# Both head pairs of a mixer as one unit of work in the three smallest query tiles of prompt attention

## The chip, the core and the metric

The kernel runs on one core of a Trainium2 chip (trn2). The metric is the device time of one execution in microseconds (us). The core has five engines that run beside each other and meet at semaphores: TensorE (PE in the profile, with its weight loads as PEld), VectorE (DVE), ScalarE (ACT), GpSimd (POOL) and SyncE (SP), which here only issues transfers.

## The reference, cut to what matters

The program is one decoder layer for a prompt of 1024 tokens and for 8 requests of 8 new tokens each. The change lies in the attention of the prompt, which has four branches. Three are those of a sparse attention with 8 query heads on 2 key heads, whose outputs are summed with gates, and the fourth is a forgetting attention with 8 heads of its own:

```python
def block(args):                       # one query tile of 128 rows
    o_n = nsa_block(...)               # g0 * compressed + g1 * selected + g2 * window
    o_f = fox_block(...)               # softmax(q k^T * scale + cq - ck) v, causal
...
lc = einsum(q, kc) * scale + bias      # compressed keys, one for 16 tokens      -> branch CMP
ls = einsum(q, kg) * scale + bias      # selected blocks (16 of 16: all)         -> branch SLC
lw = einsum(q, kw) * scale + bias      # the last 512 keys                       -> branch WIN
```

Each branch is a masked softmax over the keys up to the query, followed by a product with the values. Everything is float32.

## The kernel before, in words

`prompt_attention` handles the 1024 prompt rows in 8 query tiles of 128 rows. Query tile i needs (i + 1) * 128 keys in SLC and FOX, at most 640 in WIN, and 8i + 7 compressed keys in CMP. The tiles are not taken in the order of their number but as `TILE_ORDER = (6, 0, 5, 1, 4, 2, 3, 7)`, and all of it is done twice, in two turns of four heads per key head side: so the tiles 0, 1 and 2, the smallest three, come up six times.

The unit of work is a `Pair`: one query tile, one branch and one head pair j (0 or 1), of which `half` 0 and 1 are the two heads, on array rows 0 to 63 and 64 to 127. A tile has eight pairs, always as `CMP 0, SLC 0, SLC 1, WIN 0, CMP 1, WIN 1, FOX 0, FOX 1`; 128 pairs in all. Each goes through these steps:

- `scores` (L799, PE): one matmul for each half and 512 columns, into PSUM. A half owns two banks; a pair of at most 512 columns takes one of them, alternating with the number of the pair, and a wider one (`wide`) takes both. The score matmuls wait for the logits of all pairs up to the one before the last, or, if this pair or the one before is wide, up to the last.
- `logits` (L912; for FOX L899 for all but the diagonal 128 columns and L902 for those, with a wait between, DVE): adds the bias and takes the minimum of the negated row, for each half.
- `exps` (L956, ACT): exponential with the row sum, for each half.
- `invert` (L918, L920, DVE): the reciprocals of the sums.
- normalisation (L1021, POOL): the probabilities times the reciprocal and the gate, for each half. Ahead of WIN 0, POOL also adds the causal mask to the diagonal of the FOX bias (L1003).
- `turn` (L811, PE): transposes of 128 columns each, up to four into one of the three banks 4, 5 and 7; a pair of up to four key tiles is one chunk, a larger one two.
- `save` (L965 on ACT for half 0, L928 on DVE for half 1): the transposed probabilities to SBUF.
- `weighted_values` (L840 for CMP, SLC and WIN, both head pairs at once, 256 columns; L831 for FOX, for each head pair): the products with the values into bank 6, in two parts, one and two pairs behind the second pair of the branch. `save_out` (L972, L974, ACT) takes the results away.

The order is written out by hand. In iteration p each engine does a fixed list, in this order:

```python
# PE:   turn(p, 0); scores(p + 3); values of the pairs p - 2 and p - 1; turn(p, 1)
# DVE:  save(p, 0); logits(p + 3); save(p, 1); invert(p + 2)
# ACT:  save(p, 0); exps(p + 2, 1); save(p, 1); exps(p + 3, 0); save_out(p - 2)
# POOL: for each p in turn: wait for inverse_ready of p, normalise half 0, normalise half 1
wait_for = p.n if p.wide or (p.n and PAIRS[p.n - 1].wide) else p.n - 1     # scores
pe.wait_ge(logits_done, 2 * wait_for)
pe.wait_ge(normed, 2 * p.n + half + 1)                                     # turn
```

Transfers for the next stage, the attention of the requests, are issued by SP when the logits of the last tile (7) of the second turn are done (`logits_done`).

Of the kernel before, what the change touches and what calls it, by code (L numbers as in the profile page):

```python
# [7 lines left out]
ALU = mybir.AluOpType  # L8
ACT = mybir.ActivationFunctionType

P = 128
D = 1024
KD = D // P
T = 1024
# [7 lines left out]
NTP = T // P  # L22
# [70 lines left out]
class EarlyLayout:  # L93


    def __init__(self, arena):
# [21 lines left out]
        self.nmax, self.sums = view(arena, 24256, 4, 2, 2), view(arena, 24272, 4, 2)  # L118
# [519 lines left out]
class Pair:  # L638


    def __init__(self, n, turn, i, branch, j):
        self.n, self.turn, self.i, self.branch, self.j = n, turn, i, branch, j
        self.g = 2 * turn + j
        done = self.done = turn * NTP + TILE_ORDER.index(i)
        self.group = 4 * done + GROUPS.index(branch)
# [20 lines left out]
ORDER = ((CMP, 0), (SLC, 0), (SLC, 1), (WIN, 0), (CMP, 1), (WIN, 1), (FOX, 0), (FOX, 1))  # L666
GROUPS, BIG = (SLC, CMP, WIN, FOX), (SLC, WIN, FOX)
PAIRS = [Pair((t * NTP + y) * 8 + x, t, i, br, j)
         for t in range(2) for y, i in enumerate(TILE_ORDER) for x, (br, j) in enumerate(ORDER)]
NPAIR, AHEAD, VALUES_BEHIND = len(PAIRS), 3, 2  # L670
TURNED_BEFORE = [sum(len(q.chunks) for q in PAIRS[:n]) for n in range(NPAIR + 1)]
FOX_SPLITS = [sum(q.branch == FOX and q.i > 0 for q in PAIRS[:n]) for n in range(NPAIR + 1)]
# [10 lines left out]
def pair_no(turn, i, branch, j):  # L683
    return (turn * NTP + TILE_ORDER.index(i)) * 8 + ORDER.index((branch, j))


def prompt_attention(k, keep, io):
# [5 lines left out]
    with ExitStack() as local:  # L693
# [26 lines left out]
        def probs_of(p, half, s=0, w=None):  # L720
            return (probs_cmp if p.branch == CMP else probs)[:, p.slot, half, s:s + (p.width if w is None else w)]

        def turned_of(p):
            return (probsT_cmp if p.branch == CMP else probsT)[:, p.buf]

# [3 lines left out]
        def _(sp):  # L729
            sp.dma_start(causal[:], io["c_causal"]).then_inc(mask_in, 16)  # L730
            for turn in range(2):
                if turn:
                    sp.wait_ge(logits_done, 2 * pair_no(0, LAST_TILE, CMP, 1) + 2)
                    slc_bias(sp, at, io, turn, slc_in)
                if turn:
                    sp.wait_ge(logits_done, 2 * pair_no(0, LAST_TILE, WIN, 1) + 2)
# [4 lines left out]
                if turn:  # L741
                    sp.wait_ge(logits_done, 2 * pair_no(0, LAST_TILE, FOX, 1) + 2)
# [29 lines left out]
            sp.wait_ge(logits_done, 2 * pair_no(1, LAST_TILE, CMP, 1) + 2)  # L772
            compressor_weights(sp, ahead, io, keep.cw_in)
            sp.wait_ge(logits_done, 2 * pair_no(1, LAST_TILE, WIN, 1) + 2)
            for p in range(4):
                key_pages(sp, ahead, io, keep.first_ids, 0, p, keep.k_in)
            sp.wait_ge(logits_done, 2 * NPAIR)
# [4 lines left out]
        def _(pe):  # L782
            def scores(p):
                wait_for = p.n if p.wide or (p.n and PAIRS[p.n - 1].wide) else p.n - 1
                if wait_for > 0:
                    pe.wait_ge(logits_done, 2 * wait_for)
                pieces = split(p.width)
                for s, w in pieces:
                    cols = slice(p.k0 + s, p.k0 + s + w)
                    for half in range(2):  # L790
                        rows = slice(half * HD, (half + 1) * HD)
                        q = (keep.qfT if p.branch == FOX else keep.qT)[rows, p.g, p.i * P:(p.i + 1) * P]
                        if p.branch == FOX:
                            keys = keep.fkT[rows, p.g, cols]
# [4 lines left out]
                        mm = pe.matmul(scores_at(p, half, s, w), q, keys, start=True, stop=True)  # L799
                        if s + w == p.width:  # L800
# [1831 lines left out]
```

## Time and profile before

| | us |
|---|---|
| median of 3 runs (2605.86 to 2613.88) | 2608.65 |
| the profiled execution | 2611.62 |
| span of the profiled execution | 2609.8 |
| prompt attention inside it | about 341 to 744 |

The times of instructions below are microseconds from the start of the span. A row of the timeline gives the start, the duration, the engine, the line of the kernel, the operation with its operands and how many instructions it covers, and in brackets the idle time of the engine just before it and what ended that. A float32 matmul is recorded as several instructions: the score matmul of one piece of up to 512 columns for both halves is x4, and a transpose is x1. What an engine needs for a group is best read as the step from its start to the start of the next group, since the ends of matmuls overlap. The granted clock of TensorE is 0.998 of full speed over the span (2.4 GHz).

### The profile page before, as it was taken

What the parts mean: (1) busy time and instruction counts of PE and PEld (TensorE: products, weight loads), DVE (VectorE), ACT (ScalarE), POOL (GpSimd) and SP (SyncE); (2) the same over time, 40 slices, a digit from 0 to 9 for tenths busy, and PEclk for the clock granted to TensorE, in tenths of its full rate; (3) what the DMA queues carried; (4) which work ended last, traced back from release to release, by engine and by line L of the source; (5) the groups of instructions that cost most, each with busy time, mean ns of one, the idle gap of its engine ahead of it and who ended that gap; (6) DMA issues with size and microseconds to landing.
All of it is one profiled execution on the core that took longest, in us unless ns stands there. A gap on an engine that the chain in (4) does not pass through costs nothing.

```text
span 2609.8 us, 29562 instructions
## 1 busy us (share of the span) xinstructions
PE 2544.0 (97%) x10607; PEld 1400.4 (54%) x10607; DVE 974.1 (37%) x2734; ACT 521.0 (20%) x1306; POOL 356.3 (14%) x561
## 2 busy tenths in 40 slices
PE   9999999999989999999999999999999999999999
PEld 4554655565556675666664455555555554443443
DVE  5874246767743331101016722222222210407312
ACT  0001036656633331000002211101010110101110
POOL 0000025445540001000003400000000000202100
PEclk9999999999999999999999999999999999999999
DMA  5325430030088766111304111111111214323300
GB/s 184 93 75 174 155 123 1 1 129 2 5 209 246 223 199 202 41 32 35 102 5 95 41 33 32 43 38 32 32 32 48 78 56 162 105 97 130 127 32 32
DMA packets 198931, 227.17 MB, mean 87 GB/s; under 512 B 52551, under 2 KB 150279, under 8 KB 197263
## 3 DMA queue, kind: packets, MB, share of 16 engines
q1 hardware_dynamic: 192226, 199.85, 25.6%
q0 software_dynamic: 5424, 16.28, 1.8%
q10 hardware_dynamic: 1168, 9.58, 1.2%
q8 instruction: 65, 1.06, 0.2%
q14 instruction: 48, 0.39, 0.0%
HBM read 203.60 MB, written 37.99 MB: 93 GB/s over the span
## 4 chain that ended last, share of the span: by engine, by line
PE 61%; DVE 0%; ACT 0%; issue 0%; DVEq 0%
PE ps L2114 25%; PE ps L2164 12%; PE ps L2072 9%; PE ps L2195 5%; PE ps L2065 5%; PE ps L2092 4%; PE ps L2168 1%; PE ps L2198 0%; PE ps L2096 0%; PE ps L2121 0%; PE ps L2054 0%; PE ps L2103 0%; DVE arena L2425 0%; DVE qfT L2442 0%; ACT arena L2300 0%
## 5 line engine op out<-in xcount | busy, mean ns | idle before, releaser
L2114 PE MATMUL ps<-xT,qT 128*128 128x480 f32 (+1 forms) x2112 | 647.9, 469 | 0.0
L2114 PEld LDWEIGHTS ps<-xT,qT 128*128 128x128 f32 x2112 | 344.6, 191 | 297.6 <-issue 297.6
L2164 PE MATMUL ps<-arena 128*128 128x512 f32 x704 | 305.1, 594 | 0.0
L2072 PE MATMUL ps<-xT,arena 128*128 128x363 f32 (+1 forms) x768 | 238.1, 467 | 0.0
L2164 PEld LDWEIGHTS ps<-arena 128*128 128x128 f32 x704 | 132.8, 190 | 171.1 <-issue 170.8
L236 PE MATMUL ps<-arena,xT 128*128 128x512 f32 (+1 forms) x512 | 198.9, 551 | 1.3 <-issue 0.8
L2373 DVE TENSOR_SCALAR qfT<-qfT 128x480 f32<-128x480 f32 (+1 forms) x88 | 35.1, 420 | 435.3 <-ACT qfT L2252 435.3
L2072 PEld LDWEIGHTS ps<-xT,arena 128*128 128x128 f32 x768 | 145.4, 189 | 88.8
L956 ACT ACTIVATE arena<-arena 128x640 f32<-128x640 f32 (+15 forms) x256 | 164.8, 644 | 66.2 <-DVE arena L912 46.2
L236 PEld LDWEIGHTS ps<-arena,xT 128*128 128x128 f32 x512 | 98.1, 192 | 101.8 <-issue 94.2
L811 PE MATMUL ps<-ident,arena 128*128 128x128 f32 (+4 forms) x880 | 137.7, 284 | 10.9 <-POOL arena L1021 5.1
L1021 POOL TENSOR_SCALAR arena<-arena,gates 128x55 f32<-128x55 f32 (+15 forms) x192 | 122.8, 649 | 174.0 <-DVE arena L920 173.8
L2344 DVE TENSOR_TENSOR arena<-arena,ps 128x726 f32<-128x726 f32 (+1 forms) x24 | 21.9, 911 | 319.4 <-ACT arena L2233 319.4
L811 PEld LDWEIGHTS ps<-ident,arena 128*128 128x128 f32 (+4 forms) x880 | 91.6, 138 | 68.2 <-POOL arena L1021 29.9
L153 DVE STREAM_TRANSPOSE xT<-arena 32x256 f32<-32x256 f32 x256 | 111.6, 436 | 8.7 <-DMA arena<-in_x_all 4.8
L2195 PE MATMUL ps<-arena,xT 128*128 128x512 f32 x256 | 112.8, 593 | 0.0
L912 DVE CUSTOM_DVE_ANT_0 arena<-ps,arena 128x55 f32<-128x55 f32 (+15 forms) x192 | 96.1, 538 | 41.5 <-PE ps L799 40.5
L2092 PE MATMUL ps<-arena 128*128 128x512 f32 x256 | 110.3, 593 | 0.0
L2252 ACT COPY qfT<-ps 128x480 f32<-128x480 f32 x44 | 24.6, 558 | 427.9 <-PE ps L2114 427.9
L928 DVE COPY xT<-ps 128x512 f32<-128x512 f32 (+11 forms) x176 | 85.3, 484 | 52.0 <-PE ps L811 50.6
L799 PE MATMUL ps<-arena,qT 64*128 64x512 f32 (+11 forms) x512 | 87.5, 439 | 14.0 <-DVE arena L912 12.0
L1450 PE MATMUL ps<-ident,arena 128*128 128x128 f32 x556 | 77.5, 280 | 20.4 <-DMA arena<-in_cache_fox_kv 10.9
(288 smaller groups left out, 2594.2 us busy)
## 6 DMA issues: line engine op xcount, KB each, us to landing
arena<-in_w_ffn_down SPq DMA_DIRECT2D x66, 512.0 KB, 3.5
arena<-in_cache_fox_kv SPq DMA_DIRECT2D x72, 256.0 KB, 5.8
xT<-in_cache_fox_kv SPq DMA_DIRECT2D x56, 256.0 KB, 7.2
arena<-in_cache_nsa_kv SPq DMA_DIRECT2D x64, 192.0 KB, 4.5
qT<-in_w_ffn_up SPq DMA_DIRECT2D x22, 512.0 KB, 4.0
qT<-in_w_ffn_gate SPq DMA_DIRECT2D x22, 512.0 KB, 5.2
bias_rows<-rev_dram ACTq DMA_DIRECT2D x8, 1160.0 KB, 30.2
arena<-in_w_in SPq DMA_DIRECT2D x16, 512.0 KB, 5.4
```

Of the source, the lines that this page charges most:

```text
L153: ins = nc.vector.transpose(out[q * 32:(q + 1) * 32, :, z * 32:(z + 1) * 32], rows[z * 32:(z + 1) * 32, :].rearrange("p (c w) -> p c w", c ...
L236: mm = pe.matmul(ps[:, bank_of(i, n), 0:b - a], keep.xT[:, c, t0:t0 + m], w_rows[:, c, a:b], start=(c == 0), stop=(c == KD - 1))
L811: mm = pe.transpose(ps[0:w, turn_bank(p, c, half), x * P:(x + 1) * P], probs_of(p, half, s, w), keep.ident[:])
L912: nc.vector.tensor_tensor_reduce(dst, scores_at(p, half), bias, -1.0, FLOOR, ALU.add, ALU.min, low).then_inc(logits_done, 1)
L956: nc.scalar.activation(x, x, ACT.Exp, bias=nmax[:, p.n % 4, half, 0:1], scale=-1.0, accum_out=sums[:, p.n % 4, half:half + 1]).then_inc(ex ...
L1021: nc.gpsimd.tensor_scalar(x, x, sums[:, p.n % 4, half:half + 1], gate, ALU.mult, ALU.mult).then_inc(normed, 1)
L2065: pe.matmul(ps[:, 4 * (j % 2) + 2 + side, 0:n], at.w_branch[e][:, side, c, :], o[:, c, t0:t0 + n], start=(c == 0), stop=(c == 3))
L2072: mm = pe.matmul(ps[:, 4 * (j % 2) + side, 0:n], at.w_gate[e][:, side, c, :], x[:, c, t0:t0 + n], start=(c == 0), stop=(c == KD - 1))
L2092: mm = pe.matmul(ps[:, q + n, :], mergedT[:, c, t0:t0 + m], at.w_out[:, c, cols], start=(c == 0), stop=(c == KD - 1))
L2114: mm = pe.matmul(ps[:, 2 * (j % 3) + side, 0:n], at.w_ug[e][:, side, c, :], x[:, c, t0:t0 + n], start=(c == 0), stop=(c == KD - 1))
L2164: mm = pe.matmul(ps[:, q + h, :], hT[:, c, t0:t0 + m], at.w_down[:, load % RING, cols], start=(c == 0), stop=(c == NFF - 1))
L2195: mm = pe.matmul(ps[:, o, :], src[:, c, t0:t0 + m], w[:, c, cols], start=(c == 0), stop=(c == kk - 1))
```

## The change

In the query tiles 0, 1 and 2 the two head pairs of a branch become one `Unit`; the other tiles keep one head pair per unit, in the old order. A small tile is now four units, `CMP, SLC, WIN, FOX`, and there are 104 units in place of 128 pairs. In a unit of both head pairs:

- the score matmuls of both are issued one after the other, and `scores_ready` is counted up for a half behind the second head pair. The number of matmuls stays. Up to 256 columns a head pair (tiles 0 and 1, and CMP) both share one bank of a half; above that (SLC, WIN and FOX of tile 2, with 384 columns) the unit is `wide`, with a bank for each head pair and half, so all four banks.
- logits, exponentials and normalisations are as many as before, with one count of the semaphore for each half and not for each head pair; the guard and the reciprocal of the sums are one for both.
- a chunk of transposes is up to two key tiles of both head pairs: one chunk in the tiles 0 and 1, two (two key tiles, then one) in tile 2. A save copies both head pairs.
- the values are multiplied whole, not in two parts: CMP two units behind, the others one unit behind, and `save_out` follows one unit behind.
- CMP comes first of its tile and so opens the accumulation in bank 6.

The look-ahead stays three units, so in a small tile the scores of the next large tile are issued two or three units before it.

```diff
-class Pair:
-
...
-            self.slot, self.buf, self.freed = j, done % 2, self.group - 8 + 1
+            self.buf, self.freed = done % 2, group_no(done - 2, CMP) + 1
         else:
...
-            self.slot = (6 * done + 2 * big + j) % 3
+            self.slot = bigs % 3
             self.buf = (3 * done + big) % 2
-            before = GROUPS.index(BIG[big - 2]) + 4 * (done - (big < 2))
-            self.freed = before + 1
+            self.freed = group_no(done - (big < 2), BIG[big - 2]) + 1
         self.tiles = [(self.k0 // P + t, s, w) for t, (s, w) in enumerate(split(self.width, P))]
-        self.wide = self.width > 512
-        self.chunks = split(len(self.tiles), 4)
+        self.wide = self.width > (256 if self.both else 512)
+        self.chunks = split(len(self.tiles), 2 if self.both else 4)
...
-ORDER = ((CMP, 0), (SLC, 0), (SLC, 1), (WIN, 0), (CMP, 1), (WIN, 1), (FOX, 0), (FOX, 1))
-GROUPS, BIG = (SLC, CMP, WIN, FOX), (SLC, WIN, FOX)
-PAIRS = [Pair((t * NTP + y) * 8 + x, t, i, br, j)
...
+SINGLE = ((CMP, (0,)), (SLC, (0,)), (SLC, (1,)), (WIN, (0,)), (CMP, (1,)), (WIN, (1,)), (FOX, (0,)), (FOX, (1,)))
+DOUBLE = ((CMP, (0, 1)), (SLC, (0, 1)), (WIN, (0, 1)), (FOX, (0, 1)))
+BIG = (SLC, WIN, FOX)
+
+
+def groups_of(i):
+    return (CMP, SLC, WIN, FOX) if i < 3 else (SLC, CMP, WIN, FOX)
+
...
+    for t in range(2):
+        for i in TILE_ORDER:
+            for branch, heads in (DOUBLE if i < 3 else SINGLE):
+                units.append(Unit(len(units), t, i, branch, heads, bigs))
+                bigs += branch != CMP
+    return units
...
+WHOLE_BEHIND, HALVES_BEHIND = {CMP: (2,), SLC: (1,), WIN: (1,), FOX: (1,)}, (1, 2)
+def values_behind(p):
+
+    return WHOLE_BEHIND[p.branch] if p.both else HALVES_BEHIND
...
-        def scores_at(p, half, s=0, w=None):
-            base = half * 1024 + (0 if p.wide else (p.n % 2) * 512)
+        def scores_at(p, half, j, s=0, w=None):
+            base = half * 1024 + (0 if p.wide else (p.n % 2) * 512) + (j * (512 if p.wide else 256) if p.both else 0)
...
+        def probs_of(p, half, j, s=0, w=None):
+            w = p.width if w is None else w
+            if p.branch == CMP:
+                return probs_cmp[:, j, half, s:s + w]
+            s += 512 * j if p.both else 0
+            return probs[:, p.slot, half, s:s + w]
...
+        def turned_rows(p, t0, m, w, half):
+            heads = slice(p.heads[0], p.heads[-1] + 1)
+            return turned_of(p)[0:w, t0:t0 + m, half, heads, :].rearrange("p t j q -> p t (j q)")
+
+        def turned_bank(p, c, m, w, half):
+            return ps[0:w, turn_bank(p, c, half), 0:m * len(p.heads) * P].rearrange("p (t x) -> p t x", t=m)
...
-                wait_for = p.n if p.wide or (p.n and PAIRS[p.n - 1].wide) else p.n - 1
+                wait_for = p.n if p.wide or (p.n and UNITS_P[p.n - 1].wide) else p.n - 1
...
+                pieces = [(j, s, w) for j in p.heads for s, w in split(p.width)]
+                for j, s, w in pieces:
...
+                        mm = pe.matmul(scores_at(p, half, j, s, w), q, keys, start=True, stop=True)
+                        if (j, s, w) == pieces[-1]:
                             mm.then_inc(scores_ready, 1)
...
+                    for x, ((kt, s, w), j) in enumerate((tile, j) for tile in p.tiles[t0:t0 + m] for j in p.heads):
+                        mm = pe.transpose(ps[0:w, turn_bank(p, c, half), x * P:(x + 1) * P], probs_of(p, half, j, s, w), keep.ident[:])
...
-                cut = (last + 2) // 2
+                cut = last + 1 if p.both else (last + 2) // 2
                 some = list(enumerate(p.tiles))[part * cut:(part + 1) * cut]
+                heads = (0, 1) if p.both else (part,)
...
                         pe.wait_ge(nsa_saved, done + 1)
-                    for j in (part,):
+                    for j in heads:
...
-                    if p.branch == SLC and part == 0 and done:
+                    opens = p.branch == groups_of(p.i)[0]
+                    if opens and part == 0 and done:
                         pe.wait_ge(fox_saved, done)
...
                                            turned[0:w, x, half].rearrange("p j q -> p (j q)"),
-                                           start=(p.branch == SLC and x == 0), stop=(p.branch == WIN and x == last))
-                if part == 1 if p.branch == FOX else some[-1][0] == last:
+                                           start=(opens and x == 0), stop=(p.branch == WIN and x == last))
+                if heads[-1] == 1 if p.branch == FOX else some[-1][0] == last:
                     mm.then_inc(pv_done, 1)
...
             def values_beside(n):
-                for part in (1, 0):
-                    q = n - 1 - part
-                    if 0 <= q < NPAIR and PAIRS[q].j == 1:
-                        weighted_values(PAIRS[q], part)
+                for behind in (2, 1):
+                    q = UNITS_P[n - behind] if 0 <= n - behind < NUNIT else None
+                    if q and q.last and behind in values_behind(q):
+                        weighted_values(q, values_behind(q).index(behind))
...
+                    for x, j in enumerate(p.heads):
+                        dst = probs_of(p, half, j)
+                        low, part = nmax[:, p.n % 4, half, x, 0:1], nmax[:, p.n % 4, half, x, 1:2]
...
+                                dve.wait_ge(half_max, FOX_SPLITS[p.n] + len(p.heads) * half + x + 1)
...
+                    ins.then_inc(logits_done, 1)
...
+                nc.vector.tensor_copy(turned_rows(p, t0, m, w, 1), turned_bank(p, c, m, w, 1)).then_inc(saved_b, 1)
...
+                for n, j in enumerate(p.heads):
+                    x = probs_of(p, half, j)
+                    ins = nc.scalar.activation(x, x, ACT.Exp, bias=nmax[:, p.n % 4, half, n, 0:1], scale=-1.0,
+                                               accum_out=sums[:, p.n % 4, half, n:n + 1])
+                ins.then_inc(exp_done, 1)
...
+                nc.scalar.copy(turned_rows(p, t0, m, w, 0), turned_bank(p, c, m, w, 0)).then_inc(saved_a, 1)
...
+                for behind in (2, 1):
+                    q = UNITS_P[p.n - behind] if p.n >= behind else None
+                    if q and q.last and q.branch in (WIN, FOX) and values_behind(q)[-1] == behind:
+                        save_out(q)
...
+                    for n, j in enumerate(p.heads):
+                        x = probs_of(p, half, j)
+                        column = half * 12 + (2 * p.turn + j) * 3 + p.branch
+                        gate = 1.0 if p.branch == FOX else keep.gates[:, p.i, column:column + 1]
+                        ins = nc.gpsimd.tensor_scalar(x, x, sums[:, p.n % 4, half, n:n + 1], gate, ALU.mult, ALU.mult)
+                    ins.then_inc(normed, 1)
```

## Rows read from the trace of the kernel before

**Rows 1.** Busy time by stage: us, engines, granted clock, DMA share, GB/s.

```profile
341.50:744.40 402.90, 376.79 (x2800) 224.30 (x2800) 275.65 (x1058) 244.52 (x722) 191.00 (x281) 1.00 0.17 56
389.60:399.70 10.10, 9.77 (x102) 6.58 (x102) 6.66 (x45) 6.91 (x35) 6.26 (x14) 1.00 0.01 2
...
475.58:494.46 18.88, 18.75 (x141) 10.22 (x141) 14.78 (x63) 12.80 (x43) 10.21 (x17) 1.00 0.00 1
...
745.00:800.00 55.00, 46.59 (x358) 35.02 (x356) 14.99 (x27) 14.83 (x25) 20.54 (x51) 0.97 0.96 239
```

**Rows 2.** Timeline of PE, query tile 0 into tile 5, first turn.

```profile
390.34 1.75 PE L831 MATMUL ps<-xT,arena 128*64 128x128 f32 x28
392.02 0.44 PE L811 MATMUL ps<-ident,arena 128*128 128x128 f32 x2
...
394.39 0.44 PE L811 MATMUL ps<-ident,arena 128*128 128x128 f32 x2
394.76 0.49 PE L799 MATMUL ps<-arena,qT 64*128 64x128 f32 x4
395.18 0.44 PE L811 MATMUL ps<-ident,arena 128*128 128x128 f32 x2
...
399.33 0.44 PE L811 MATMUL ps<-ident,arena 128*128 128x128 f32 x2
399.70 1.56 PE L799 MATMUL ps<-arena,qT 64*128 64x512 f32 x8
...
403.19 1.56 PE L799 MATMUL ps<-arena,qT 64*128 64x512 f32 x8 [0.98 <-DVE arena L912]
...
406.68 1.35 PE L799 MATMUL ps<-arena,qT 64*128 64x512 f32 x8 [1.58 <-DVE arena L912]
```

**Rows 3.** Timeline of PE, query tile 1 into tile 4, first turn.

```profile
432.97 0.70 PE L799 MATMUL ps<-arena,qT 64*128 64x256 f32 x4
433.60 1.53 PE L831 MATMUL ps<-xT,arena 128*64 128x128 f32 x24
...
438.66 0.66 PE L811 MATMUL ps<-ident,arena 128*128 128x128 f32 x4
439.24 0.70 PE L799 MATMUL ps<-arena,qfT 64*128 64x256 f32 x4
...
444.79 1.35 PE L799 MATMUL ps<-arena,qT 64*128 64x512 f32 x8
...
447.81 1.35 PE L799 MATMUL ps<-arena,qT 64*128 64x512 f32 x8 [0.49 <-DVE arena L912]
...
450.82 1.35 PE L799 MATMUL ps<-arena,qT 64*128 64x512 f32 x8 [0.74 <-DVE arena L912]
```

**Rows 4.** Timeline of PE, query tile 2 into tile 3, first turn.

```profile
475.78 0.92 PE L799 MATMUL ps<-arena,qT 64*128 64x384 f32 x4
...
491.68 0.87 PE L811 MATMUL ps<-ident,arena 128*128 128x128 f32 x6
492.49 1.13 PE L799 MATMUL ps<-arena,qT 64*128 64x512 f32 x4
...
494.46 1.13 PE L799 MATMUL ps<-arena,qT 64*128 64x512 f32 x4
```

**Rows 5.** Timeline of DVE, tile 2: logits of one pair, then of FOX.

```profile
482.00 0.56 DVE L912 CUSTOM_DVE_ANT_0 arena<-ps,arena 128x384 f32<-128x384 f32 x1 [0.28 <-PE ps L799]
...
482.48 0.55 DVE L912 CUSTOM_DVE_ANT_0 arena<-ps,arena 128x384 f32<-128x384 f32 x1
...
483.91 0.42 DVE L899 CUSTOM_DVE_ANT_0 arena<-ps,arena 128x256 f32<-128x256 f32 x1
...
484.65 0.42 DVE L899 CUSTOM_DVE_ANT_0 arena<-ps,arena 128x256 f32<-128x256 f32 x1
```

**Rows 6.** Timeline of POOL, tile 2: the diagonal and a normalisation.

```profile
479.42 1.27 POOL L1003 TENSOR_TENSOR arena<-arena 128x512 f32<-128x512 f32 x1
481.02 1.30 POOL L1021 TENSOR_SCALAR arena<-arena,gates 128x384 f32<-128x384 f32 x2 [0.33 <-DVE arena L920]
```

More of the change, by code:

```diff
@@ L635, in _, with __init__ @@
             nc.vector.tensor_copy(keep.vc[0:CMP_N, :], ps[0:CMP_N, HIGH, HD:HD + P]).then_inc(kcvc_saved, 1)
-class Pair:
-    def __init__(self, n, turn, i, branch, j):
-        self.n, self.turn, self.i, self.branch, self.j = n, turn, i, branch, j
-        self.g = 2 * turn + j
+class Unit:
+    def __init__(self, n, turn, i, branch, heads, bigs):
+        self.n, self.turn, self.i, self.branch, self.heads = n, turn, i, branch, heads
+        self.both, self.first, self.last = len(heads) == 2, heads[0] == 0, heads[-1] == 1
         done = self.done = turn * NTP + TILE_ORDER.index(i)
-        self.group = 4 * done + GROUPS.index(branch)
+        self.group = group_no(done, branch)
         if branch == CMP:
             self.k0, self.width = 0, 8 * i + 7
-            self.slot, self.buf, self.freed = j, done % 2, self.group - 8 + 1
+            self.buf, self.freed = done % 2, group_no(done - 2, CMP) + 1
         else:
@@ new lines, in group_no, with units_in_order @@
+def group_no(done, branch):
+    return 4 * done + groups_of(TILE_ORDER[done % NTP]).index(branch)
+def units_in_order():
+    units, bigs = [], 0
+    for t in range(2):
[4 more added lines that the diff above has]
+    return units
+UNITS_P = units_in_order()
+NUNIT, AHEAD = len(UNITS_P), 3
+TURNED_BEFORE = [sum(len(q.chunks) for q in UNITS_P[:n]) for n in range(NUNIT + 1)]
@@ L675 @@
+FOX_SPLITS = [sum(2 * len(q.heads) for q in UNITS_P[:n] if q.branch == FOX and q.i > 0) for n in range(NUNIT + 1)]
+WHOLE_BEHIND, HALVES_BEHIND = {CMP: (2,), SLC: (1,), WIN: (1,), FOX: (1,)}, (1, 2)
+def values_behind(p):
+    return WHOLE_BEHIND[p.branch] if p.both else HALVES_BEHIND
 TURN_BANKS = (4, 5, 7)
@@ L680, in turn_bank, with unit_no @@
     return TURN_BANKS[(2 * (TURNED_BEFORE[p.n] + c) + half) % 3]
-def pair_no(turn, i, branch, j):
-    return (turn * NTP + TILE_ORDER.index(i)) * 8 + ORDER.index((branch, j))
+def unit_no(turn, i, branch, j):
+    return next(q.n for q in UNITS_P if (q.turn, q.i, q.branch) == (turn, i, branch) and j in q.heads)
 def prompt_attention(k, keep, io):
@@ L791, in scores @@
                         rows = slice(half * HD, (half + 1) * HD)
-                        q = (keep.qfT if p.branch == FOX else keep.qT)[rows, p.g, p.i * P:(p.i + 1) * P]
+                        q = (keep.qfT if p.branch == FOX else keep.qT)[rows, g, p.i * P:(p.i + 1) * P]
                         if p.branch == FOX:
-                            keys = keep.fkT[rows, p.g, cols]
+                            keys = keep.fkT[rows, g, cols]
                         elif p.branch == CMP:
@@ L867, in _ @@
             pe.wait_ge(queries_b, 1)
[L868 removed]
+            for p in UNITS_P:
                 if p.n == 1:
@@ L885, in logits @@
                     if p.branch in (SLC, CMP):
-                        dve.wait_ge(slc_in[p.j], 32 * p.turn + 32)
-                    elif p.j == 0:
+                        for j in p.heads:
+                            dve.wait_ge(slc_in[j], 32 * p.turn + 32)
+                    elif p.first:
                         dve.wait_ge(win_in if p.branch == WIN else fox_in, 64 * p.turn + 64)
-                if p.j == 0 and p.branch == FOX:
+                if p.first and p.branch == FOX:
                     dve.wait_ge(diag_ready, p.done + 1)
@@ L1001, in set_diagonal @@
                 if p.done % NTP >= 2:
-                    pool.wait_ge(logits_done, 2 * pair_no(p.turn, TILE_ORDER[p.done % NTP - 2], FOX, 1) + 2)
+                    pool.wait_ge(logits_done, 2 * unit_no(p.turn, TILE_ORDER[p.done % NTP - 2], FOX, 1) + 2)
                 nc.gpsimd.tensor_tensor(diag_fox[:, p.done % 2], bias_fox[:, :, :, p.i * P:(p.i + 1) * P].rearrange("p h j n -> p (h j) n"),
@@ L1013, in _ @@
             pool.wait_ge(mask_in, 16)
-            for p in PAIRS:
-                if p.branch == WIN and p.j == 0:
+            for p in UNITS_P:
+                if p.branch == WIN and p.first:
                     set_diagonal(p)
```

130 lines of the change are left out of this document (50 added, 80 removed).

## The prediction

> **What bounds the kernel now.** I read the busy time by stage first, then the timeline of PE around each small tile, then DVE's and POOL's for the steps that PE might wait for. In the busy times the reader is to see that prompt attention takes 402.9 us, that PE is busy in 376.79 of them, and that in tile 0 it is so for 9.77 of 10.10 us and in tile 2 for 18.75 of 18.88 us, at a granted clock of 1.00 (2.4 GHz) [rows 1]. DVE, the next, has 14.78 of 18.88 us. So the small tiles are bound by PE, and a part of PE's time is the price of small groups. The exception is the end of the tiles 0 and 1: there PE issues the scores of the next large tile, which take all score banks, and stands 0.98 and 1.58 us, or 0.49 and 0.74 us, waiting for DVE's logits [rows 2, 3]. Nothing stands there in tile 2, since tile 3 has 512 columns and its scores alternate between banks [rows 4].
>
> **Length of the small tiles.** SLC(5) is SLC of tile 5, and so on. Take as the end of a tile the start of the third large score group behind it. From the first scores issued in the tile's CMP 0 that is 450.82 - 432.97 = 17.85 us for tile 1 [rows 3] and 494.46 - 475.78 = 18.68 us for tile 2 [rows 4]; in tile 0 those scores come one step of 0.42 us ahead of the FOX values at 390.34, so 406.68 - 389.9 = 16.8 us [rows 2].
>
> **What the change does to PE's steps.** Nothing of the matrix work goes; a group's fixed part goes. A group's step is its duration less some 0.07 us.
> - Scores: 128 columns of one head pair step 0.42 us (394.76 to 395.18) [rows 2]. What a piece of 128 more columns adds shows between 256 and 384 columns, 0.92 - 0.70 = 0.22 us [rows 3, 4]. A unit of two is thus 0.42 + 0.21 = 0.63 against 0.84 us, and so with 256 columns (0.63 + 0.43 = 1.06 against 1.26) and 384 (0.85 + 0.64 = 1.49 against 1.70). With CMP some 0.8 us a tile.
> - Transposes: two step 0.37 us (394.39 to 394.76) [rows 2], four 0.58 (438.66 to 439.24) [rows 3], six 0.81 (491.68 to 492.49) [rows 4]: 0.11 each and 0.15 for the group. Four groups less in the tiles 0 and 1: 0.6 us. In tile 2 a big unit has two chunks (eight and four), 1.03 + 0.58 = 1.61 against 2 x 0.81, so nothing but 0.15 for CMP.
> - Values: no longer split, 0.1 us a group; 0.2 to 0.3 us in tile 2.
> That is 1.4 us of PE's work in tiles 0 and 1 and some 1.2 us in tile 2.
>
> **What it does to the waits.** Half the iterations mean that the scores of the next tile come earlier against the small tile's remaining work. For tile 0, from the rows, PE is busy back to back. The prefetched scores of three units make CMP's turn later by about 0.5 us, at 390.2. Then: turn CMP 0.5, scores FOX 0.65, values of FOX(6) 1.68 (390.34 to 392.02) [rows 2], turn SLC 0.58, scores CMP(5) 0.33, values 1.68, turn WIN 0.58: SLC(5)'s scores start at 396.2 to 396.4 against 399.70. The next two follow at the distance that DVE's logits set, 3.49 us (399.70 to 403.19) [rows 2]. PE's own work between them, 1.49 scores, 1.1 values of CMP and SLC, 0.58 transposes of FOX, is 3.2 us and just fits. The third is at 403.4 against 406.68: **3.25 us** gained, 1.4 of fixed parts, 1.3 of the wait at the end and the rest short waits inside the tile, which PE no longer meets.
>
> Tile 1, in the same way: CMP turn at about 433.1, then 0.7, 1.06, 1.46 (432.97 group's values, 433.60, less 0.07) [rows 3], 1.03, 0.33, 1.46 and WIN's transposes. Here the transposes wait for POOL. Its normalisation of SLC ends near 436.3, the diagonal takes 1.27 [rows 6], and four normalisations of WIN at 0.55 end near 440.1 (0.55 is an estimate between 0.65 for 384 columns [rows 6] and the shorter ones). SLC(4)'s scores start at 440.65. Now PE itself sets the distance: 1.28 + 1.6 values + 1.03 transposes = 3.9 us, then 3.02 (444.79 to 447.81) [rows 3]: third group at 447.6 against 450.82, **3.2 us**.
>
> Tile 2 is the doubtful one. Its SLC, WIN and FOX scores fill all four banks, so each must wait until the last one's logits are done. DVE needs 0.48 us for each head and head pair, 1.93 for the unit (482.00 to 482.48), for FOX 0.74 and 2.96 (483.91 to 484.65) [rows 5]. On PE the values and transposes behind a score group cover it: behind SLC's 2.8 us, of tile 4 (covered); behind WIN's 1.8 us (a wait of about 0.2 us); behind FOX's 2.3 us, values 1.25 and transposes 1.03 (a wait of about 0.7 us). These three are my counts of groups by the steps above. DVE's queue costs more: `invert` of WIN stands behind the logits of FOX and comes at 482.3, POOL then takes 2 x 1.30 [rows 6], and PE has WIN's second half of transposes at 484.95, some 0.4 us late. Without any wait the tile would be 16.7 us: 18.68 less 1.2 of fixed parts and less 0.7 of short waits for POOL inside it, such as the 0.3 us that end at each normalisation. Of the new waits some hide each other; I take 0.8 us, so 17.5 against 18.68: **1.2 us** gained. Bounds: 2.0 gained with no wait, 4.9 lost (second rival).
>
> Saves: one of 512 columns for two of 256; they and the exponentials lie on ACT beside PE (6.91 of 10.10 us busy in tile 0 [rows 1]) and cost nothing on the path; were they bare, ACT in tile 2 would be 12.8 of 17.5 us, still no bound. The longer hand-over (a half is announced after both head pairs) is in the schedule above; POOL's queue holds only the next units behind it. No DMA is issued in another place; SP's waits keep their events.
>
> **Behind the stage.** The loads of the next stage are issued on the logits of the last tile, and until then DMA is at 0.17 of its time [rows 1]. The 55 us that follow are bound by DMA at 0.96, which starts with those issues; so the gain is passed on, since everything slides.
>
> **Sum.** 2 turns x (3.25 + 3.2 + 1.2) = 15.3 us. The profiled execution is 2611.62 (span 2609.8 and 1.8 around it), 3.0 over the median: 2611.62 - 15.3 = 2596.3 for a like execution, and 2608.65 - 15.3 = **2593.4** for the median.
>
> **Rivals.**
> 1. *The small tiles gain in part.* If the waits inside tiles 0 and 1 come back (POOL's four normalisations of a unit in a row, against two now) but the fixed parts go, it is 2 x (1.4 + 1.4 + 0) = 5.6: 2603. For it: POOL ended idle times of PE already in these tiles. Against: POOL has 6.26 of 10.10 us busy [rows 1].
> 2. *All four banks give up the overlap.* If nothing covers the logits, tile 2 has PE idle for 1.93 + 1.93 + 2.96 = 6.8 us, less 1.2 of work and 0.7 of waits that go: 4.9 lost, so 2 x (6.45 - 4.9) = 3.1 gained, 2605.5. For it: this is just how PE stands at the large tiles [rows 2]. Against: there PE had too little other work; here it has. The Trainium skill (Perfetto Trace Analysis, Matmuls) says that independent matmul groups should rotate through PSUM banks so that the eviction of one overlaps the next; by that rule, which speaks against the wide units, this rival would be the likely one. The trace agrees with it at tile 5.
> 3. *Slower: the ring of a wide unit closes.* In tile 2 each unit runs turn 1.03, scores 1.49, logits 2.96, the second turn and save 1.0, invert 0.4, normalisation 2.6 one behind the other: 9.5 us where two pairs take 4.6. Three such units lose 14.7 us a turn: 29.4 less 12.9 of the other tiles, 16.5 slower, 2625. It decides from a loss of 2.2 us for each wide unit on. Against it: the look-ahead of three units, which lets the steps of neighbours lie beside each other.
> 4. *Absorbed.* The stage behind waits for something that does not slide (a load issued early): 2608. Against: DMA's mean share of 0.17 in this stage [rows 1], and loads that are issued by its last tile.
>
> **Chances.** Forecast 0.74, rival 1 0.07 and rival 2 0.07, rival 3 0.07, rival 4 0.05. About 0.3% (7.8 us) is what a measurement of this kernel can tell from none. Rivals 1, 2 and 4 lie within it, 0.19; from their edges 0.01 goes to either side: faster 0.75, same 0.17, slower 0.08. The forecast's own range reaches 2 x 0.8 us further down for tile 2 and 2 x 1.3 for the waits for POOL and for PE's own distance in tile 1, and some 6 us up, if each small tile meets one more wait of 1 us: 2589 to 2600. To leave out no more than 2 in 10 it takes in rivals 1 and 2: **2587 to 2606**.
>
> **What would show it.** In the trace of the changed kernel: score groups x8 of 2 x 128 columns stepping about 0.63 us; the score group of tile 5 at 3.2 us earlier against tile 0's start, tile 4's likewise; idle time of PE before WIN's and FOX's scores in tile 2 of a few tenths, against 2 us in rival 2; PE's second half of WIN's transposes released by POOL in tile 2. Wrong would be the forecast if PE stood over 1 us before each wide group of tile 2, if POOL ended more than 1.5 us of idle time in tile 0 or 1, or if the stage behind did not start earlier by 15 us.

## The result, and the profile after

| | median us | ratio to before, 95% interval |
|---|---|---|
| before (13 runs beside it) | 2611.07 | |
| the changed kernel (13 runs) | 2616.72 | 1.0019 [1.0012, 1.0027] |

The change made the kernel slower by 0.19%, 5.65 us, where 15.3 us less were forecast. It is within the 0.3% called no difference ahead, but the interval lies clear of 1. The profiled execution took 2616.97 us with a span of 2615.2 us, at a mean granted clock of 0.993 against 0.998.

The stage as a whole, then stretches in the tiles 1 and 2 of the first turn, with the columns of [rows 1]:

```profile
341.00:744.00 403.00, 368.09 (x2720) 225.90 (x2718) 259.50 (x991) 237.53 (x701) 190.58 (x279) 0.97 0.16 53
...
434.00:442.00 8.00, 5.97 (x73) 4.55 (x70) 4.58 (x27) 5.05 (x19) 4.19 (x7) 1.00 0.01 2
442.00:448.00 6.00, 5.21 (x26) 2.73 (x28) 2.26 (x6) 2.02 (x9) 3.22 (x7) 0.72 0.01 3
481.60:486.40 4.80, 1.22 (x12) 0.84 (x8) 2.88 (x17) 1.43 (x5) 1.74 (x2) 0.83 0.00 0
486.40:491.80 5.40, 5.33 (x36) 4.84 (x36) 1.79 (x12) 2.92 (x10) 3.06 (x5) 0.52 0.01 3
```

PE was busy in 1.22 of the 4.80 us from 481.6 us on, and then 5.33 of 5.40 us at a clock of 0.52: it first stood and then worked at half speed (1.2 of 2.4 GHz; the clock had already fallen within the wait, at about 484.7). In tile 1 the same follows in small. Nowhere in this stage does the kernel before show a clock under 1.00 [rows 1].

PE's timeline shows both at the instruction (in the changed kernel L837 are the scores, L849 the transposes, L870 the values of FOX, L880 the other values). In tile 1 of the changed kernel:

```profile
438.56 1.53 PE L870 MATMUL ps<-xT,arena 128*64 128x128 f32 x24
442.38 0.66 PE L849 MATMUL ps<-ident,arena 128*128 128x128 f32 x4 [2.29 <-POOL arena L1065]
443.45 0.86 PE L849 MATMUL ps<-ident,arena 128*128 128x128 f32 x4 [0.42 <-POOL arena L1065]
444.25 2.50 PE L837 MATMUL ps<-arena,qT 64*128 64x512 f32 x8
```

The same timeline of the changed kernel in tile 2:

```profile
478.97 1.56 PE L837 MATMUL ps<-arena,qfT 64*128 64x384 f32 x8
480.46 1.31 PE L870 MATMUL ps<-xT,arena 128*64 128x128 f32 x20
481.70 1.11 PE L849 MATMUL ps<-ident,arena 128*128 128x128 f32 x8
486.47 0.64 PE L837 MATMUL ps<-arena,qT 64*128 64x31 f32 x4 [3.65 <-DVE arena L943]
487.04 2.40 PE L870 MATMUL ps<-xT,arena 128*64 128x128 f32 x20
489.37 2.57 PE L849 MATMUL ps<-ident,arena 128*128 128x128 f32 x12
491.87 1.13 PE L837 MATMUL ps<-arena,qT 64*128 64x512 f32 x4
```

In tile 1 PE waits 2.29 us for POOL's normalisation of WIN, and the score group behind it takes 2.50 us where its like takes 1.35 [rows 3]. In tile 2 it waits 3.65 us for the last FOX logits (L943), and the values and transposes behind take 2.40 and 2.57 us. Who was late there is on two more timelines of the changed kernel. POOL's:

```profile
479.50 2.60 POOL L1065 TENSOR_SCALAR arena<-arena,gates 128x384 f32<-128x384 f32 x4 [2.80 <-DVE arena L961]
482.07 1.27 POOL L1045 TENSOR_TENSOR arena<-arena 128x512 f32<-128x512 f32 x1
486.82 2.60 POOL L1065 TENSOR_SCALAR arena<-arena,gates 128x384 f32<-128x384 f32 x4 [3.48 <-DVE arena L961]
```

And DVE's:

```profile
483.37 0.42 DVE L940 CUSTOM_DVE_ANT_0 arena<-ps,arena 128x256 f32<-128x256 f32 x1 [3.65 <-POOL arena L1045]
...
486.53 0.18 DVE L961 RECIPROCAL arena<-arena 128x4 f32<-128x4 f32 x1
```

The FOX scores were ready at 480.53, but DVE began their logits at 483.37, released by POOL's L1045: 2.8 us late. That line adds the causal mask to the diagonal of the FOX bias, and it stands in POOL's queue between SLC's four normalisations and WIN's. Before, FOX 0's logits came in the iteration of WIN 0, when the diagonal was done: in tile 2 at 480.69, and the logits began at 483.91 [rows 5, 6]. In a tile of four units they come in CMP's iteration. DVE stands 2.8 to 3.7 us for it in each of the six small tiles and in no large one; `invert` of WIN is queued behind the logits, and so POOL begins WIN at 486.8. POOL itself stands idle for 3.48 us between the diagonal and WIN, so it is not the 1.27 us of POOL's own time that make WIN late, but DVE's wait for them.

**Length by tile.** The save of the sparse branches (L972 before, L1013 now) of each large tile bounds a small one and the large one behind it. From ACT's timeline of the kernel before (tiles 6, 5, 4 and 3 of the first turn):

```profile
389.83 0.36 ACT L972 COPY qT<-ps 128x256 f32<-128x256 f32 x1
...
433.02 0.36 ACT L972 COPY qT<-ps 128x256 f32<-128x256 f32 x1
...
475.94 0.36 ACT L972 COPY qT<-ps 128x256 f32<-128x256 f32 x1
...
518.87 0.35 ACT L972 COPY qT<-ps 128x256 f32<-128x256 f32 x1
```

The same saves of the changed kernel:

```profile
393.77 0.35 ACT L1013 COPY qT<-ps 128x256 f32<-128x256 f32 x1
...
435.10 0.35 ACT L1013 COPY qT<-ps 128x256 f32<-128x256 f32 x1
...
479.56 0.35 ACT L1013 COPY qT<-ps 128x256 f32<-128x256 f32 x1
...
524.97 0.35 ACT L1013 COPY qT<-ps 128x256 f32<-128x256 f32 x1
```

| us, from save to save | before | changed | diagonal early (first run below) |
|---|---|---|---|
| with tile 0 (6 to 5) | 43.19 | 41.33 | 40.07 |
| with tile 1 (5 to 4) | 42.92 | 44.46 | 40.47 |
| with tile 2 (4 to 3) | 42.93 | 45.41 | 40.86 |

A row holds the small tile and the large one behind it, and in the large one the scores of the next small tile are prefetched. So what tile 2's prefetched scores cost, 1.9 us in tile 4 (25.06 before, 26.97 changed), stands in the row of tile 1, which without them is 0.4 us shorter than before and not 1.5 longer. To this comes 0.84 us a turn, ahead of the first save, for tile 0's scores, now issued for both head pairs (29.21 us from tile 7 to tile 6 before, 30.05 now). So a turn is 3.0 us longer and both 6.0, which is the 5.65 us of the medians.

### The profile page after: what moved, and what is told of

The parts are those of the page before. It is cut to its first block, busy times and chain, and to the rows that moved or that the text cites. A ratio compares the mean times of both kernels' runs of the same rounds, so it can differ in the third digit from the quotient of the medians.

```text
span 2615.2 us, 29416 instructions
## 1 busy us (share of the span) xinstructions
PE 2544.2 (97%) x10607; PEld 1409.7 (54%) x10607; DVE 959.8 (37%) x2668; ACT 515.5 (20%) x1288; POOL 356.9 (14%) x561
## 4 chain that ended last, share of the span: by engine, by line
PE 61%; DVE 0%; ACT 0%; issue 0%; DVEq 0%
PE ps L2159 25%; PE ps L2209 12%; PE ps L2117 9%; PE ps L2240 5%; PE ps L2110 5%; PE ps L2137 4%; PE ps L2213 1%; PE ps L2243 0%; PE ps L2141 0%; PE ps L2166 0%; PE ps L2099 0%; PE ps L2148 0%; DVE arena L2470 0%; DVE qfT L2487 0%; ACT arena L2345 0%
## 5 line engine op out<-in xcount | busy, mean ns | idle before, releaser
L849 PE MATMUL ps<-ident,arena 128*128 128x128 f32 (+4 forms) x880 | 134.0, 286 | 17.6 <-POOL arena L1065 13.2
L849 PEld LDWEIGHTS ps<-ident,arena 128*128 128x128 f32 (+4 forms) x880 | 94.1, 141 | 64.7 <-issue 28.7
L837 PE MATMUL ps<-arena,qT 64*128 64x512 f32 (+11 forms) x512 | 85.9, 445 | 16.6 <-DVE arena L943 7.8
```

Source lines behind the costliest of these rows:

```text
L849: mm = pe.transpose(ps[0:w, turn_bank(p, c, half), x * P:(x + 1) * P], probs_of(p, half, j, s, w), keep.ident[:])
```

## The experiments

Each ratio is against the kernel before, run on the same chip in the same rounds; its median was 2612.93 us beside the early diagonal, both kernels with two tiles and the early diagonal in pairs, 2611.60 beside the filled wait, the doubled, the late and the everywhere early diagonal, and 2613.17 beside the last two.

**Diagonal early in the small tiles.**

```diff
-                if p.branch == WIN and p.first:
+                if p.first and p.branch == (CMP if p.both else WIN):
                     set_diagonal(p)
```

> The changed kernel with one edit: in the small tiles POOL adds the mask to the FOX diagonal ahead of the normalisation of CMP, not ahead of that of WIN. Theory D (the FOX logits of a small tile, now issued in CMP's iteration, stand behind POOL's normalisation of SLC and the diagonal; DVE's wait of 2.8 to 3.7 us holds up the inverse of WIN and PE, and PE's idle time lets its clock fall): the six waits of DVE go, no stretch of the small tiles is at half clock, and the time falls to the forecast, about 2596 us against 2611 for the kernel before. Rival B (the four score banks of tile 2 give up the overlap): PE still stands over 2 us before the scores behind FOX in tile 2 and its clock still falls there; only the tiles 0 and 1 gain, about 2604 us. Rival C (two normalisations more in a row on POOL are what PE waits for): time stays within 3 us of the changed kernel's 2616.7.

Measured 2597.08 us against 2612.93, ratio 0.9940 [0.9926, 0.9954]: 15.85 us faster than before. DVE waits for POOL's diagonal nowhere, and no small tile has a fall of the clock (all lengths stand in the table above). PE's timeline of this kernel in tile 2:

```profile
474.55 1.10 PE L849 MATMUL ps<-ident,arena 128*128 128x128 f32 x8
476.62 0.41 PE L837 MATMUL ps<-arena,qT 64*128 64x31 f32 x4 [0.97 <-DVE arena L943]
476.96 1.31 PE L870 MATMUL ps<-xT,arena 128*64 128x128 f32 x20
478.20 1.09 PE L849 MATMUL ps<-ident,arena 128*128 128x128 f32 x8
479.60 0.66 PE L849 MATMUL ps<-ident,arena 128*128 128x128 f32 x4 [0.31 <-POOL arena L1065]
480.19 1.13 PE L837 MATMUL ps<-arena,qT 64*128 64x512 f32 x4
```

From POOL's and DVE's timelines of the same kernel, the normalisation of SLC and the first of FOX's logits:

```profile
472.35 2.59 POOL L1065 TENSOR_SCALAR arena<-arena,gates 128x384 f32<-128x384 f32 x4 [2.80 <-DVE arena L961]
...
473.52 0.42 DVE L940 CUSTOM_DVE_ANT_0 arena<-ps,arena 128x256 f32<-128x256 f32 x1 [0.95 <-PE ps L837]
```

The logits of FOX start at 473.52, released by the scores and not by POOL, a microsecond after POOL has begun SLC. PE's wait for the last of them is 0.97 us, not 3.65. Theory D stands; rival B wanted over 2 us there, and rival C the old time.

At the end of tile 0 PE's wait for the score banks is shorter than before, but not gone. PE's timeline of this kernel:

```profile
400.75 1.56 PE L837 MATMUL ps<-arena,qT 64*128 64x512 f32 x8 [0.18 <-DVE arena L953]
...
404.24 1.35 PE L837 MATMUL ps<-arena,qT 64*128 64x512 f32 x8 [1.00 <-DVE arena L953]
```

These are 0.18 and 1.00 us for 0.98 and 1.58 [rows 2]; at the end of tile 1 it is none and 0.31 us for 0.49 and 0.74 [rows 3].

**Units of both head pairs in the tiles 0 and 1 alone, with the late and with the early diagonal.**

```diff
-            for branch, heads in (DOUBLE if i < 3 else SINGLE):
+            for branch, heads in (DOUBLE if i < 2 else SINGLE):
...
-    return (CMP, SLC, WIN, FOX) if i < 3 else (SLC, CMP, WIN, FOX)
+    return (CMP, SLC, WIN, FOX) if i < 2 else (SLC, CMP, WIN, FOX)
```

> The changed kernel, but only the tiles 0 and 1 have units of both head pairs; tile 2 is as before, and no unit takes four banks at 384 columns. Theory D: tile 2 gives back the 2.5 us a turn that it lost, tile 0 still gains 1.9 and tile 1 still loses 1.5 with its fall of the clock: 2609 to 2612 us, no difference to before that can be told. Rival B (the four banks are the cause of the loss): all of the loss goes and the tiles 0 and 1 show their gain, 2603 us or less. Rival C: like theory D.

> Both edits: units of both head pairs in the tiles 0 and 1 alone, and the diagonal ahead of CMP there. Theory D: 2 x (3.25 + 3.2) = 12.9 us faster than before, 2598 us, some 2 us slower than with three tiles and the early diagonal. Rival B: the same 2598, but faster than with three tiles by 5 us or more. Rival C: near the run with two tiles and the late diagonal, 2610 us.

Measured 2608.80 us, ratio 0.9987 [0.9978, 0.9996], and 2598.63 us, ratio 0.9945 [0.9933, 0.9957]. The first is 4 us faster than before, and 8 us faster than the changed kernel; the second cannot be told from the run with three tiles (2597.08). So the tiles 0 and 1 give all of the gain, if the diagonal is early, and the four banks of tile 2 are by themselves neither the loss nor a gain. The late one missed its expectation, if narrowly: it was to show no difference to before, and its interval lies just clear of 1. The expectation charged tile 1 with the 1.9 us that tile 2's prefetched scores cost in tile 4, and they are gone here: by the saves tile 1's row is 0.4 us shorter than before in the first turn and 2.0 in the second.

The late diagonal also showed, unplanned, what the clock costs. The wait of tile 1 is the same in both turns, 2.25 us; behind it the clock fell in the first and not in the second. PE's timeline of the kernel with two tiles and the late diagonal, in both turns:

```profile
442.52 0.66 PE L849 MATMUL ps<-ident,arena 128*128 128x128 f32 x4 [2.25 <-POOL arena L1065]
443.59 0.84 PE L849 MATMUL ps<-ident,arena 128*128 128x128 f32 x4 [0.41 <-POOL arena L1065]
444.36 2.51 PE L837 MATMUL ps<-arena,qT 64*128 64x512 f32 x8
...
449.66 1.35 PE L837 MATMUL ps<-arena,qT 64*128 64x512 f32 x8
...
632.62 0.66 PE L849 MATMUL ps<-ident,arena 128*128 128x128 f32 x4 [2.25 <-POOL arena L1065]
633.69 0.66 PE L849 MATMUL ps<-ident,arena 128*128 128x128 f32 x4 [0.41 <-POOL arena L1065]
634.28 1.35 PE L837 MATMUL ps<-arena,qT 64*128 64x512 f32 x8
...
638.17 1.35 PE L837 MATMUL ps<-arena,qT 64*128 64x512 f32 x8
```

From the transposes to the second score group it is 449.66 - 442.52 = 7.14 us in the one and 638.17 - 632.62 = 5.55 us in the other: 1.6 us for one fall.

**PE's wait filled.** The changed kernel, in which SLC's first chunk of transposes is done again, into the same bank:

```diff
-                    for x, ((kt, s, w), j) in enumerate(...):
-                        mm = pe.transpose(...)
+                    for again in range({1: 3, 2: 4}.get(p.i, 1) if p.both and p.branch == SLC and c == 0 else 1):
+                        for x, ((kt, s, w), j) in enumerate(...):
+                            mm = pe.transpose(...)
                     mm.then_inc(turned, 1)
```

> The changed kernel with PE's wait filled: in the tiles 1 and 2 the first chunk of SLC's transposes is done three (tile 1) or four times (tile 2) and counted once, about 1.8 and 2.7 us of PE's work inside waits of 2.3 and 3.7 us. It does not shorten the wait's end. Theory D with the clock: the four stretches at half clock go, and with them the 1.6 us (tile 1) and 2.3 us (tile 2) that they cost a turn: 7.8 us faster than the changed kernel, 2609. Rival (the clock costs nothing, since PE would wait anyway, or the filling delays what comes after): the same as the changed kernel or slower, 2617 to 2622.

Measured 2611.26 us, ratio 0.9999 [0.9991, 1.0008]: 5.5 us faster than the changed kernel, with more work on PE. No stretch of the small tiles is at half clock. PE's timeline of this kernel in tile 2:

```profile
478.74 3.71 PE L850 MATMUL ps<-ident,arena 128*128 128x128 f32 x32
483.52 0.41 PE L837 MATMUL ps<-arena,qT 64*128 64x31 f32 x4 [1.07 <-DVE arena L944]
483.86 1.31 PE L871 MATMUL ps<-xT,arena 128*64 128x128 f32 x20
485.11 1.09 PE L850 MATMUL ps<-ident,arena 128*128 128x128 f32 x8
```

DVE's wait is still 3.66 us and PE still stands until the logits come, but only 1.07 us in one piece, and the values and transposes behind take 1.31 and 1.09 us. By the saves, the stretch with tile 1 is 1.6 us shorter and that with tile 2 1.8: 6.8 us in both turns against 7.8 expected. The rest of what the late diagonal costs, 2611.3 - 2597.1 = 14 us by the medians (12.8 by the saves), is standing time, as far as these two runs divide it.

**The diagonal twice.** The suspected cost doubled in the changed kernel:

```diff
+                nc.gpsimd.tensor_tensor(diag_fox[...], bias_fox[...], causal[...], ALU.add).then_inc(diag_first, 1)
+                pool.wait_ge(diag_first, p.done + 1)
                 nc.gpsimd.tensor_tensor(diag_fox[...], bias_fox[...], causal[...], ALU.add).then_inc(diag_ready, 1)
```

> The changed kernel with the diagonal's addition done twice in a row on POOL, in all 16 tiles. Theory D: DVE's waits for it in the six small tiles grow by 1.3 us each, some 4.1 to 5.0 us, all of it on the path in the tiles 1 and 2 and most of it in tile 0, and no stretch at half clock goes: 6 to 10 us slower than the changed kernel, 2623 to 2627. If the diagonal were beside the path (rival C), no more than 2 us.

Measured 2641.75 us, ratio 1.0111 [1.0095, 1.0126]: 25 us slower than the changed kernel, where 6 to 10 were expected. The waits of DVE did grow as expected, to 4.17, 4.48 and 5.00 us. Most of the surplus lies where I had not looked: in the large tiles PE waits for POOL's normalisation of WIN 0, behind the diagonal, as well, and in the tiles 4 and 3 the clock now falls there too. PE's timeline of this kernel in tile 4:

```profile
468.58 0.66 PE L850 MATMUL ps<-ident,arena 128*128 128x128 f32 x4 [1.14 <-POOL arena L1070]
469.44 0.66 PE L850 MATMUL ps<-ident,arena 128*128 128x128 f32 x4 [0.20 <-POOL arena L1070]
470.02 2.34 PE L838 MATMUL ps<-arena,qfT 64*128 64x512 f32 x8
472.29 2.17 PE L881 MATMUL ps<-xT,arena 128*64 128x256 f32 x12
```

The stretches from a small tile's save to that of the large tile behind it are 1.3 to 2.9 us longer each, 6.8 a turn. The small tiles' own are 1.4 to 3.3 us longer, where the wait alone grew by 1.3; in tile 1 of the first turn the clock stays at half from about 446.3 to 456.7.

**Pairs only, with a late diagonal.** The kernel before, no unit of two head pairs:

```diff
-                if p.branch == WIN and p.j == 0:
+                if p.branch == WIN and p.j == 1:
```

> The kernel before, pairs alone, with the diagonal two pairs later, ahead of WIN 1's normalisation. FOX 0's logits, issued in WIN 0's iteration, then stand behind two normalisations that were not ahead of them. Theory D: DVE waits for POOL in all 16 tiles and the kernel gets slower without any unit of two head pairs, by about 1 us a tile or more, 2625 to 2650, with stretches at half clock in the small tiles. Rival (it takes the longer units and the halved number of iterations to make that wait bare): within 3 us of before.

Measured 2644.27 us, ratio 1.0122 [1.0106, 1.0138]. DVE waits 1.5 to 1.9 us for POOL in all 16 tiles, as in tile 5 on DVE's timeline of this kernel:

```profile
424.49 0.82 DVE L899 CUSTOM_DVE_ANT_0 arena<-ps,arena 128x640 f32<-128x640 f32 x1 [1.53 <-POOL arena L1003]
```

The clock falls in five of the six small tiles. The flaw is one of order and needs no unit of two.

**The diagonal early in the kernel before, and in all tiles of the changed one.** In both the diagonal goes ahead of CMP's normalisation everywhere (`p.branch == CMP`).

> The kernel before with the diagonal moved ahead of the normalisation of CMP 0 in all tiles. Theory D: DVE never waited for it here, since FOX 0's logits come in the iteration of WIN 0; the time stays within 3 us of before, 2608 to 2614. Rival E (its place costs the kernel before as well, and a gain of the first run would not be the changed kernel's): faster than before by 5 us or more.

> The changed kernel with the diagonal ahead of CMP's normalisation in all 16 tiles, not in the small ones alone. Theory D: DVE waits for it nowhere; the large tiles never waited for it, but POOL's queue is freer ahead of WIN 0, where PE waited for POOL by some tenths: 0 to 4 us faster than with the early diagonal in the small tiles alone (2597), that is 2593 to 2597. Against: 1.3 us ahead of CMP 0 and SLC 0 might delay those, then up to 3 us slower.

Measured 2609.36 us, ratio 0.9987 [0.9979, 0.9996], and 2596.72 us, ratio 0.9942 [0.9929, 0.9955]. The first is 3.6 us faster than before, a little more than the 3 us allowed: the diagonal's place cost the kernel before a little, but not what the first run gained. By the saves only the tiles 2 and 3 are shorter there, 0.6 us a turn. The second cannot be told from the first run; in its trace only the large tile 3 is 0.9 us shorter a turn (24.49 to 23.57).

**Tile 2 alone, with the early diagonal there.**

```diff
-            for branch, heads in (DOUBLE if i < 3 else SINGLE):
+            for branch, heads in (DOUBLE if i == 2 else SINGLE):
...
-                if p.branch == WIN and p.first:
+                if p.first and p.branch == (CMP if p.both else WIN):
```

> Units of both head pairs in tile 2 alone, with the diagonal ahead of CMP there; all else as before. The forecast's term for this tile is 1.2 us a turn, so 2.4 us faster than before, 2609. By the traces of the runs with two and with three tiles it is 0.2 us a turn: no difference to before. Rival B (four banks without overlap): slower by 5 us or more, 2617.

Measured 2612.28 us against 2613.17, ratio 0.9997 [0.9988, 1.0006]: no difference. From save to save, tile 4 is 1.9 us longer (25.06 to 26.96), tile 2 2.8 shorter (19.16 to 16.38), and tile 3 0.7 longer (23.77 to 24.49), both turns alike: 0.2 us gained. In tile 3 PE now waits for POOL's normalisation of WIN 0, which stands behind that tile's own diagonal; the kernel before shows no such wait there. PE's timeline of this kernel:

```profile
502.46 1.41 PE L849 MATMUL ps<-ident,arena 128*128 128x128 f32 x8 [0.62 <-POOL arena L1065]
```

With the diagonal early in all tiles this wait is gone, and tile 3 takes 23.57 us, against 23.30 in the kernel before with the diagonal early in all tiles. So the same order of POOL's queue makes some 0.4 of the 0.7 us, and 0.3 stay without a cause.

**WIN's reciprocals ahead of FOX's logits.** On top of the diagonal early in all tiles:

```diff
                 save(p, 0)
+                sooner = p.both and p.branch == CMP
+                if sooner:
+                    invert(UNITS_P[p.n + AHEAD - 1])
                 if p.n + AHEAD < NUNIT:
                     logits(UNITS_P[p.n + AHEAD])
...
-                if p.n + AHEAD - 1 < NUNIT:
+                if not sooner and p.n + AHEAD - 1 < NUNIT:
                     invert(UNITS_P[p.n + AHEAD - 1])
```

> The changed kernel with the diagonal ahead of CMP in all tiles (2596.7 us) and one more edit: in CMP's iteration of a small tile DVE takes WIN's sums and their reciprocals ahead of FOX's logits, not behind them. If the inverse of WIN behind four logits of FOX is what still makes PE wait in the tiles 1 and 2 (0.39 and 0.31 us for POOL), those go and it is 1 to 1.5 us faster, 2595 to 2596. If FOX's logits are the longer chain (PE waits 0.97 us for them in tile 2), the exponentials that the inverse needs hold them up and nothing is gained, or 1 us is lost.

Measured 2597.48 us, ratio 0.9940 [0.9926, 0.9953], the same as without it. By the saves tile 1 is 0.6 us shorter, but tile 2 is 2.1 longer: the wait for FOX's logits doubles and the clock falls behind it, as PE's timeline of this kernel shows:

```profile
477.54 0.41 PE L837 MATMUL ps<-arena,qT 64*128 64x31 f32 x4 [2.01 <-DVE arena L943]
477.88 1.31 PE L870 MATMUL ps<-xT,arena 128*64 128x128 f32 x20
479.13 2.82 PE L849 MATMUL ps<-ident,arena 128*128 128x128 f32 x12
```

## Why the prediction was wrong

**The step that failed** is the schedule's start of FOX's logits. The forecast had DVE begin them as soon as the scores were there ("for FOX 0.74 and 2.96", covered by 2.3 us of PE's work), and named the diagonal only as 1.27 us that delay POOL's next normalisation: "Its normalisation of SLC ends near 436.3, the diagonal takes 1.27". It listed what POOL's queue holds behind the diagonal, but not who waits for the diagonal itself, though the kernel says so (`dve.wait_ge(diag_ready, p.done + 1)`). With half the units, the unit three behind CMP is FOX, and its logits moved from the fourth and fifth of eight iterations to the first of four, past POOL's SLC and diagonal. Expected start in tile 2: as soon as the scores end; measured: 2.8 us later, in 3.65 us of DVE's waiting (0.95 with the early diagonal, for the scores alone), and PE's wait ahead of the scores behind FOX 3.65 us where the forecast had 0.7. That the early diagonal alone turns +5.65 into -15.85 us shows it.

**A second term was missing: the clock.** No rival priced PE's standing at more than its length. The falls behind the waits cost 5.5 us (the filled run; 6.8 by the saves) of the 19.6 us that lie between the changed kernel and the run with the early diagonal. The Trainium skill (TensorE: Matmul & The Clock Gate, HAM oscillation) describes this pattern on a kernel whose PE waits some 3 to 5 us for transfers between bursts of matmuls: it is throttled, and the next burst starts at half clock. The traces agree for the wait of 3.65 us, and the fill removes the fall. The fall behind 2.29 us (and 0.42 us close behind it) shows that here shorter waits than those of the page were enough.

**What was right.** With the diagonal early, the mechanism and nearly the sum are as forecast: PE's fixed parts go and its waits at the end of the tiles 0 and 1 are filled in part, as reckoned (tile 0's from 2.56 to 1.18 us, where 1.3 were to go), 15.85 us by the medians [12 to 19], 13.6 by the saves, against 15.3. Score groups of 128 columns for both head pairs are x8 of 0.71 us (step 0.65, forecast 0.63). By tile, the tiles 0 and 1 gave 7.5 less 0.84 us of prefetch, 6.6 a turn (the run with two tiles and the early diagonal; forecast 6.45). Tile 2 gave 0.2, not 1.2: the term was mis-sized. The waits inside it that I knew of came to 0.97 and 0.31 us where 0.2, 0.7 and 0.4 were listed and 0.8 taken, and "18.68 less 1.2" and less 0.7 is 16.8 and not 16.7. Tile 4 is 1.9 us longer with the prefetched scores, against 2.8 that tile 2 is shorter; the forecast set a price on prefetched scores in tile 0 (0.5 us) and none in tile 2. And tile 3 loses 0.7 us that I had not reckoned with, more than half of it to the diagonal again. "The stage behind slides" was right too: the difference inside the stage, 6.0 us, arrives at the end as 5.65.

**The rivals.** Rival 2 (four banks give up the overlap) fell with the tile 2 run, which is level with before: PE had other work to put there, as the forecast said against the rule that it cites. Rival 3 had the right sign and in part the right ring, with invert and normalisation behind FOX's logits, but for another reason; it took 14.7 us a turn for tile 2's units, and the changed kernel is 3.0 us a turn slower in all. Rival 1 named waits for POOL, and its sign was there: POOL ended 2.29 us of PE's idle time in tile 1, over the 1.5 us that the forecast allowed. But its reason, four normalisations in a row, is not the cause: with the early diagonal they stay in a row, and the wait is 0.39 us. Rival 4 (absorbed) fell with the same run, since its gain arrives at the end.

**Left open.** Why the clock fell behind one of two equal waits of 2.25 us was not tried. Nor was what part of tile 2's missing 1 us the prefetched scores in tile 4 take and what part the waits inside tile 2.

## What to carry to other kernels

When the number of iterations changes and the look-ahead stays a count of units, list for every instruction that moves what it waits for, and find each producer's place in its own queue: a small instruction of a third engine (here 1.27 us of a mask) that had slack by order alone may now be the one that all stand behind. Moving it two units ahead in its queue, an edit of one line, turned the loss into the whole gain. And a wait on PE is to be priced at its length and, in dense work, with the chance that what follows runs at half clock; breaking the wait into pieces with useless work can be cheaper than standing (5.5 us here).

## What the runs showed of the hardware

The granted clock of PE fell to 0.5 (1.2 GHz), for some 3 to 7 us, in the wait of 3.65 us and behind waits of 2.29 us, of 2.25 us (once of two times) and of 2.01 us (the last run); with the late diagonal in the kernel before also behind 1.91 and 2.02 us and, once of two times, 1.71 us. It did not in the kernel before behind its waits of 0.98 and 1.58 us [rows 2], nor where 3.65 us of waiting were cut to 1.07. The longest wait alone does not decide: with the diagonal twice it fell in tile 4 behind waits of 1.14, 0.20 and 0.20 us close together, PE being busy in 8.46 of the 10.00 us from 460 to 470, while the kernel before had PE busy in 7.39 of the 10.00 us from 399.7 on, and no fall. I have no rule from it. One such fall in dense work costs 1.6 us. All kernels also show two to five such stretches elsewhere in the program, not in the same places in each profiled execution (about 238, 344, 780 or 1010 us, among others); whether they make the scatter of the runs was not tested.
